# Expert blocks of 64 and of 128 rows in pairs, in the two-layer trunk's mixture of experts

## The chip, the cores and the metric

One Trainium2 chip, of which the kernel uses one core. The metric is the device time of one execution in microseconds (us), as the median of several; less is better. Its engines: TensorE (PE; PEld are its loads of stationary operands), VectorE (DVE), ScalarE (ACT), GpSimd (POOL) and SyncE (SP), which here only issues DMAs.

## The reference

Two layers over 1024 tokens of width 1024. In each, three mixers in parallel (a gated chunk mixer, a convolution, attention with latent keys) are normed and projected by W_o; then comes the mixture of experts, then a gated embedding per layer (gate W_g, projection e of p). All is float32. The change is in the mixture:

```python
t = m.reshape(-1, D)                       # 1024 tokens
g_idx = argmax(t @ wg + bg)                # 1 of 4 groups
topv, topi = top_k(softmax(elog of the group), 2)   # 2 of its 8 experts
flat_e = (g_idx[:, None] * 8 + topi).reshape(-1)    # 2048 choices, 32 experts
counts = bincount(flat_e, length=32)
padded = (counts + 127) // 128 * 128       # whole blocks of 128 rows
def expert_block(tok_b, w_b, e):           # for each block of 128 rows
    xb = t[tok_b]
    hb = silu(xb @ w_gate[e]) * (xb @ w_up[e])      # 1024 -> 256
    return (hb @ w_down[e]) * w_b[:, None]          # 256 -> 1024
```

On average an expert has 64 choices. The weights of one expert are three matrices of 1 MB. On the kernel's inputs the reference's routing gives, in layer 0, one expert with 134 choices, 16 with 65 to 117 and 15 with 25 to 62; in layer 1, 14 with 67 to 110 and 18 with 35 to 62.

## The kernel before

Every engine runs a program of its own, tied to the others by semaphores; the loop over the two layers is outside. A layer has the mixers, W_o with the norm and the router's logits, and then:

*Routing.* The end of W_o leaves the logits. VectorE computes the top two and the block lists in a chain of small instructions, each of which waits for the one before (`link`, L1417). TensorE counts choices per expert and ranks every choice by products with a triangle (L1915 to L1919), then turns the block counts into starts (`nb_col`, L1923). VectorE makes from them the block and the slot of each choice, 2 x 16 one-hot matrices (`hots`, L1487 to L1492), and TensorE multiplies these into the list of tokens of each block (L1932). The expert of each block is found on one partition by comparing the ends with a row of numbers, `le` and `owner` (L1499 to L1501). The cells of row 0 (`cells`) hold the owners, the number of blocks and running counts of the semaphores; the last is written at L1520. In the meantime TensorE works on e = p W_p in four calls of `project` (L1899); ScalarE copies e out and stores it in 16 DMAs over the two layers. SP, POOL, ACT, DVE and PE each wait for the cells and load five registers (`counters`, L455) before the blocks begin.

*Blocks.* All engines walk through the blocks with `block_loop` (L442), three to a lap, since weights and inputs have three slots. SP loads gate and up (L609, L610) into a slot as soon as gate_up of the block before the last but one is done and, after its down, the down weights (L614); the loads of the second block on also wait for the stores of e, whose buffer slot 1 takes. POOL gathers a block's rows of m by an indirect DMA (L783) into `x_blk` and scatters its output from `y_blk` into `choice_outputs` (L810); padding rows have an index out of bounds and are not moved. TensorE's order is written out by hand (L1982):

```python
guarded(pe, b < n, lambda: gate_up(m, *here))
guarded(pe, b + 1 < n, lambda: turn_x(m + 1, *nxt))
guarded(pe, b <= n, lambda: down(m - 1, *last))
guarded(pe, b < n, lambda: turn_h(m))
```

gate_up (L1957) is 8 products of 128 stationary columns (the block's rows) with 512 moving ones (gate and up), each of which the trace shows as two records; turn_x (L1948) is 8 transposes of the next block's rows; down (L1967) 4 products of 128 x 512 of the block before; turn_h (L1974) 2 transposes. ACT and DVE take the results out of PSUM: x in halves (L1048, L1527), silu and product (L1052, L1532, L1534), the hidden rows (L1056), y in halves (L1062, L1539). The evacuation of y waits until the store of the block before has landed, for there is one `y_blk`. After the blocks, SP waits for all stores, fetches each token's two rows, and the last part of the layer adds them to h.

## Time and profile before

| | |
|---|---|
| median of 3 runs | 2376.19 us (2371.58 to 2377.60) |
| profiled execution | 2380.11 us, span 2378.4 us |
| PE busy | 2184.1 us (92%), 8095 instructions |
| PEld / DVE / ACT / POOL busy | 1217.5 / 1100.9 / 594.8 / 369.1 us |
| mean granted clock of TensorE | 0.956 of full |
| DMA | 358.73 MB, mean 151 GB/s |
| experts' stages (first gate_up to last down) | 676 to 1056 us, and 1860 to 2229 us |

A matmul's record overlaps its neighbours, so busy time of a group is less than its count times the mean. A window of the trace gives each engine's busy time in it, the granted clock and the share of the 16 DMA engines' time, which can exceed 1 a little where packets overlap.

### The profile page before, as it was taken

What the parts mean: (1) busy time and instruction counts of PE and PEld (TensorE: products, weight loads), DVE (VectorE), ACT (ScalarE), POOL (GpSimd) and SP (SyncE); (2) the same over time, 40 slices, a digit from 0 to 9 for tenths busy, and PEclk for the clock granted to TensorE, in tenths of its full rate; (3) what the DMA queues carried; (4) which work ended last, traced back from release to release, by engine and by line L of the source; (5) the groups of instructions that cost most, each with busy time, mean ns of one, the idle gap of its engine ahead of it and who ended that gap; (6) DMA issues with size and microseconds to landing.
All of it is one profiled execution on the core that took longest, in us unless ns stands there. A gap on an engine that the chain in (4) does not pass through costs nothing.

```text
span 2378.4 us, 32689 instructions
## 1 busy us (share of the span) xinstructions
PE 2184.1 (92%) x8095; PEld 1217.5 (51%) x8095; DVE 1100.9 (46%) x2442; ACT 594.8 (25%) x1325; POOL 369.1 (16%) x545
## 2 busy tenths in 40 slices
PE   5999699999979999978979997999999799999698
PEld 2555477755534444434435554776555344444344
DVE  1488878754411121115425888787535121111253
ACT  2333233422211111111123332443213111111111
POOL 1222100011022222210013221000110222222100
PEclk9999799999889999998989997999998899999799
DMA  6011321001399999955300114210014999999422
GB/s 230 14 27 26 104 92 28 15 27 62 143 319 334 328 318 304 316 181 203 108 27 14 27 26 134 62 41 1 27 62 156 321 320 330 329 314 326 159 94 88
DMA packets 242022, 358.73 MB, mean 151 GB/s; under 512 B 22708, under 2 KB 190980, under 8 KB 241924
## 3 DMA queue, kind: packets, MB, share of 16 engines
q1 hardware_dynamic: 220900, 315.60, 39.7%
q0 software_dynamic: 18720, 33.60, 3.7%
q10 hardware_dynamic: 2304, 8.39, 0.9%
q8 instruction: 42, 0.69, 0.1%
q14 instruction: 56, 0.46, 0.1%
HBM read 324.48 MB, written 67.63 MB: 165 GB/s over the span
## 4 chain that ended last, share of the span: by engine, by line
PE 83%; DVE 6%; issue 5%; DMA 3%; ACT 1%; SPq 1%; DVEq 0%; POOL 0%; ACTq 0%; POOLq 0%
PE ps L1648 32%; PE ps L1957 19%; PE ps L1967 9%; PE ps L1805 4%; PE ps L1835 4%; PE ps L1617 2%; PE ps L1948 2%; PE ps L1819 2%; PE ps L1905 2%; PE ps L1737 2%; DMA h<-in_x_dram 1%; PE ps L1746 1%; DMA region_c<-in_moe_w_up_dram 1%; DVE neg_max L1355 1%; PE ps L1717 1%
## 5 line engine op out<-in xcount | busy, mean ns | idle before, releaser
L1648 PE MATMUL ps<-region_b,region_c 128*128 128x512 f32 x1024 | 453.3, 599 | 2.7 <-DVE region_c L1164 2.7
L1648 PE MATMUL ps<-region_a,region_c 128*128 128x512 f32 (+1 forms) x768 | 325.0, 578 | 14.9 <-ACT region_c L879 14.9
L1957 PE MATMUL ps<-region_c,region_a 128*128 128x512 f32 x704 | 314.4, 600 | 7.7 <-DMA region_c<-in_moe_w_up_dram 6.8
L1648 PEld LDWEIGHTS ps<-region_b,region_c 128*128 128x128 f32 x1024 | 194.1, 193 | 230.1 <-issue 229.6
L1532 DVE SCALAR_TENSOR_TENSOR region_a<-region_a,ps 128x256 f32<-128x256 f32 x65 | 27.4, 421 | 456.5 <-ACT region_a L1052 456.5
L1648 PEld LDWEIGHTS ps<-region_a,region_c 128*128 128x128 f32 x768 | 147.3, 195 | 175.8 <-issue 175.8
L1957 PEld LDWEIGHTS ps<-region_c,region_a 128*128 128x128 f32 x704 | 132.2, 193 | 159.0 <-issue 159.0
L1805 PE MATMUL ps<-region_c 96*128 96x512 f32 (+3 forms) x384 | 160.6, 530 | 0.0
L1967 PE MATMUL ps<-region_c,region_a 128*128 128x512 f32 x352 | 158.4, 593 | 0.7 <-DVE region_c L1539 0.7
L1957 PE MATMUL ps<-region_a 128*128 128x512 f32 x336 | 147.7, 592 | 0.0
L1835 PE MATMUL ps<-region_c,region_a 128*128 128x64 f32 x1152 | 146.8, 274 | 0.0
L1835 PEld LDWEIGHTS ps<-region_c,region_a 128*128 128x128 f32 x1152 | 143.1, 197 | 0.0
L1617 PE MATMUL ps<-ident,region_c 128*128 128x128 f32 x496 | 70.8, 292 | 76.0 <-DVE region_c L1148 60.0
L1052 ACT ACTIVATE region_a<-ps 128x256 f32<-128x256 f32 x65 | 25.0, 385 | 436.4 <-PE ps L1957 436.4
L991 ACT ACTIVATE region_a<-ps,neg_max 128x128 f32<-128x128 f32 (+7 forms) x128 | 94.9, 742 | 126.3 <-DVE neg_max L1355 124.8
L1539 DVE COPY region_c<-ps 128x512 f32<-128x512 f32 x65 | 44.9, 691 | 161.1 <-PE ps L1967 151.8
L1355 DVE TENSOR_REDUCE neg_max<-ps 128x1 f32<-128x128 f32 (+7 forms) x128 | 96.4, 754 | 45.9 <-PE ps L1808 45.1
L1617 PEld LDWEIGHTS ps<-ident,region_c 128*128 128x128 f32 x496 | 62.3, 150 | 101.4 <-DVE region_c L1148 73.5
L1819 PE MATMUL ps<-ident,region_a 128*128 128x128 f32 x576 | 89.1, 283 | 22.0 <-ACT region_a L991 22.0
L1957 PEld LDWEIGHTS ps<-region_a 128*128 128x128 f32 x336 | 62.2, 190 | 70.3 <-issue 70.3
L1967 PEld LDWEIGHTS ps<-region_c,region_a 128*128 128x128 f32 x352 | 63.6, 190 | 64.9 <-issue 64.9
L1819 PEld LDWEIGHTS ps<-ident,region_a 128*128 128x128 f32 x576 | 64.2, 145 | 52.4 <-ACT region_a L991 35.2
(292 smaller groups left out, 2810.3 us busy)
## 6 DMA issues: line engine op xcount, KB each, us to landing
region_c<-in_moe_w_gate_dram SPq DMA_DIRECT2D x44, 1024.0 KB, 9.1
region_c<-in_moe_w_up_dram SPq DMA_DIRECT2D x44, 1024.0 KB, 11.9
region_c<-in_moe_w_down_dram SPq DMA_DIRECT2D x44, 1024.0 KB, 5.7
region_a<-in_moe_w_gate_dram SPq DMA_DIRECT2D x21, 1024.0 KB, 9.7
region_a<-in_moe_w_up_dram SPq DMA_DIRECT2D x21, 1024.0 KB, 12.3
region_a<-in_moe_w_down_dram SPq DMA_DIRECT2D x21, 1024.0 KB, 5.6
region_c<-choice_outputs SPq DMA_DIRECT2D x32, 512.0 KB, 4.4
qk_heads<-gains SPq DMA_DIRECT2D x32, 384.0 KB, 4.2
```

Of the source, the lines that this page charges most:

```text
L991: nc.scalar.activation(prob[j % 2][:, 0:n], banks(2 * (j % 2))[:, 0:n], ACT.Exp, bias=neg_max[:, j % 2:j % 2 + 1], accum_out=denom[:, j:j ...
L1355: v.tensor_reduce(neg_max[:, j % 2:j % 2 + 1], banks(2 * (j % 2))[:, 0:(j + 1) * P], AX.X, ALU.max, negate=True).then_inc(*X_max.next(f"ma ...
L1617: ins = T(bank(b + k // 4, P * (k % 4), P * (k % 4) + P), src[:, P * k:P * k + P], ident[:, :])
L1648: ins = mm(dst, lhsT[:, k, :], w[:, k, a:b], start=(k == 0), stop=(k == KD - 1))
L1737: ins = mm(bank(half, 0, w), cnT[:, k, :], w_uq[:, k, w * half:w * half + w], start=(k == 0), stop=(k == 1))
L1805: mm(bank(b + c // 512, 0, w), q, k_ring[u][0:QK, c:c + w], start=True, stop=not last, skip_group_check=True)
L1819: ins = T(bank(4 + k // 4, P * (k % 4), P * (k % 4) + P), prob[j % 2][:, P * k:P * k + P], ident[:, :])
L1835: ins = mm(bank(6 + j % 2, 0, HEAD), prob_t[j % 2][:, k, :], vals[:, k, head, :], start=(k == 0), stop=(k == j))
L1905: ins = mm(bank(2 + 2 * u + half), pT[:, i, u, k, :], ple_p[:, k, 512 * half:512 * half + 512], start=(k == 0), stop=(k == 1))
L1948: ins = T(bank(k // 4, P * (k % 4), P * (k % 4) + P), x_blk[s][:, P * k:P * k + P], ident[:, :])
L1957: ins = mm(bank(2), xT[:, k, :], w_gu[s][:, k, :], start=(k == 0), stop=(k == KD - 1))
L1967: ins = mm(bank(4 + half), hid_t[:, k, :], w_dn[s][:, k, 512 * half:512 * half + 512], start=(k == 0), stop=(k == 1))
```

## The change

Each expert's choices are cut into full blocks (65 to 128 rows) and at most one small block (up to 64). Blocks are run in pairs, a small one first and then a full one; the number of pairs is half the number of blocks, rounded up, or the number of full ones if that is more. Small blocks beyond the number of pairs go into full places; places left over are void blocks with the weights of some expert and no rows to store that anyone reads. In a small block gate and up are computed with 64 stationary columns twice, `tile_position=(0, 0)` and `(0, 64)`: the two halves of the array's columns take 256 different moving columns each and write partitions 0 to 63 and 64 to 127. Down is split in the same way, the hidden rows need one transpose, and a small output is stored as 128 half rows from a buffer of its own, `y_half`; each of the two output buffers has its semaphore. The laps have six blocks. Owners come from three products on TensorE, placed between the halves of `project(1)`; SP starts the first loads after the owners, ahead of `counters`; slot 1 lies now where slot 2 was, so the third load waits for the stores of e. Block keys carry several fields that are cut out again with shifts and masks. The diff, cut to its core (ACT's and DVE's evacuations take `small` and half the width in the same way):

```diff
+            with eng.Fori(0, LAPS) as i:
+                def six():
+                    for u in range(6):
+                        b = 6 * i + (1 + u)
+                        step(b, ((1 + u) % 3, 2 * i + (1 + u) // 3), ((2 + u) % 3, 2 * i + (2 + u) // 3), (u % 3, 2 * i + u // 3),
+                             u % 2 == 0, 3 * i + u // 2)
+                guarded(eng, 6 * i < n, six)
...
-                prev, n, used = counters(sp, l, passed)
...
+                sp.wait_ge(*K_vec.after(l, "owner_i"))
+                settle(sp, passed)
                 for b in range(3):
-                    if b == 1:
+                    if b == 2:
                         for u in range(2):
                             sp.wait_ge(e_stored[u], 16 * PAIRS * l + 16 * PAIRS + 16)
                         settle(sp, passed)
                     load_dn(load_gu(b, b), b)
...
+                prev, n, half = counters(sp, l, passed, halves=True)
...
+                    rows = HALF if small else P
...
+                        out=x_blk[s][0:rows], out_offset=None, in_=m_dram,
+                        in_offset=bass.IndirectOffsetOnAxis(ap=idx_ring[0:rows, s:s + 1], axis=0),
...
+                gp.wait_ge(*K_vec.after(l, "rows_half"))
+                settle(gp, passed)
...
-                            in_=y_blk, in_offset=None, bounds_check=2 * SEQ - 1, oob_is_err=False).then_inc(y_stored, 16)
+                            out=y_halves if small else y_rows,
+                            out_offset=bass.IndirectOffsetOnAxis(ap=out_ring[:, k:k + 1], axis=0),
+                            in_=y_half if small else y_blk, in_offset=None, bounds_check=2 * VOID if small else VOID,
+                            oob_is_err=False).then_inc(y_stored[k], 16)
...
+                    act.wait_ge(y_stored[0 if small else 1], (half + i) * 16)
...
+                link(v.tensor_scalar(cnt[:, 1:2], cnt[:, 0:1], HALF - 1, None, ALU.add), "cnt_full")
+                link(v.tensor_scalar(cnt[:, 2:3], cnt[:, 0:1], P - 1, None, ALU.add), "cnt_all")
+                link(v.tensor_scalar(cnt[:, 3:5], cnt[:, 1:3], 7, None, ALU.logical_shift_right), "cnt_nb")
+                link(v.tensor_copy(nb_f[:, 0:2], cnt[:, 3:5]), "nb_f")
+                link(v.tensor_tensor(nb_f[:, 2:3], nb_f[:, 1:2], nb_f[:, 0:1], ALU.subtract), "n_half")
+                link(v.tensor_scalar(nb_cols[0:NE, 0], ones_b[0:NE, :], nb_f[:, 0:1], None, ALU.mult), "col_full")
+                link(v.tensor_scalar(nb_cols[0:NE, 1], ones_b[0:NE, :], nb_f[:, 2:3], None, ALU.mult), "col_half")
...
+                link(v.tensor_copy(ends, bank(6, 64, 64 + 4 * NE).rearrange("p (a e) -> p a e", a=4)), "start_f")
+                link(v.tensor_copy(cols[:, 0:2], ps[0:NE, 6, 192:194]), "cols_f")
+                link(v.tensor_tensor(both, n_full, n_half, ALU.add), "both")
+                link(v.tensor_scalar(quarter, both, 0.5, 0.25, ALU.mult, ALU.add), "quarter")
+                link(v.tensor_scalar(whole, quarter, ROUND, None, ALU.add), "whole")
+                link(v.tensor_scalar(n_pairs, whole, ROUND, n_full, ALU.subtract, ALU.max), "pairs")
...
+                link(v.tensor_scalar(cols[:, 2:3], cols[:, 1:2], n_pairs[0:NE], 0.0, ALU.subtract, ALU.max), "behind")
+                link(v.tensor_scalar(le[:, 0], nth_row, cols[:, 0:1], None, ALU.is_ge), "le_full")
+                link(v.tensor_scalar(le[:, 1], nth_row, cols[:, 2:3], n_full[0:NE], ALU.subtract, ALU.is_ge), "le_late")
+                link(v.tensor_scalar(le[:, 2], nth_row, cols[:, 1:2], None, ALU.is_ge), "le_half")
...
+                link(v.tensor_scalar(shift, n_full, n_pairs, -float(NE), ALU.subtract, ALU.subtract), "from_pairs")
+                link(v.tensor_scalar(keys[:, 0], start_half, n_pairs, shift, ALU.is_ge, ALU.mult), "moved")
+                link(v.scalar_tensor_tensor(keys[:, 1], end_full, 15.0, start_full, ALU.mult, ALU.add), "key_full")
+                link(v.tensor_tensor(keys[:, 2], start_half, keys[:, 0], ALU.add), "key_half")
+                link(v.scalar_tensor_tensor(keys[:, 3], keys[:, 2], 512.0, keys[:, 1], ALU.mult, ALU.add), "key")
...
+                link(v.tensor_scalar(dest, dest_f, float(SEQ), None, ALU.add), "dest_i")
...
+                for k, (name, right, mask) in enumerate((("slot", 0, P - 1), ("nth", 7, 7), ("is_half", 10, 1), ("end_full", 11, NE - 1),
+                                                         ("nr_half", 16, POS - 1))):
+                    link(v.tensor_scalar(fields_i[:, k], dest, right, mask, ALU.logical_shift_right, ALU.bitwise_and), name)
+                link(v.tensor_copy(fields, fields_i), "fields")
...
+                v.wait_ge(*K_pe.after(l, "owners"))
+                link(v.tensor_copy(owner, ps[0:1, 6, 256:256 + POS]), "owner_f")
+                link(v.tensor_scalar(cells[0:1, 0:POS].rearrange("p (r a) -> p a r", a=2), owner.rearrange("p (a r) -> p a r", a=2),
+                                     NE - 1, None, ALU.bitwise_and), "owner_i")
+                link(v.tensor_tensor(shared, fields[:, 3], fields[:, 1], ALU.add), "nr_full")
+                link(v.scalar_tensor_tensor(apart, fields[:, 4], -float(NE - 8), shared, ALU.add, ALU.subtract), "apart")
+                link(v.tensor_tensor(swap, apart, fields[:, 2], ALU.mult), "swap")
+                link(v.scalar_tensor_tensor(blk_f, swap, float(NE - 8), shared, ALU.add, ALU.add), "blk")
...
-                link(v.tensor_tensor(le, ends[0:1, 1].unsqueeze(1).to_broadcast([1, MAXB1, NE]),
-                                     iota[0:1, 0:MAXB1].unsqueeze(2).to_broadcast([1, MAXB1, NE]), ALU.is_le), "le")
-                link(v.tensor_reduce(owner, le, AX.X, ALU.add), "owner")
...
+                link(v.tensor_scalar(total, n_pairs[0:1], 2.0, None, ALU.mult), "n_blocks")
...
+                v.tensor_scalar(by_kind(idx), kinds, 3 * SEQ - 1, None, ALU.bitwise_and).then_inc(*K_vec.next("list_i"))
+                v.tensor_copy(cells[0:1, POS + 6:POS + 7], n_pairs[0:1]).then_inc(*K_vec.next("n_cell"))
+                v.tensor_copy(cells[0:1, POS + 4:POS + 5], total).then_inc(*K_vec.next("cells"))
+                v.tensor_copy(by_kind(out_idx)[:, 1], kinds[:, 1]).then_inc(*K_vec.next("rows_full"))
+                v.tensor_scalar(by_kind(out_idx)[:, 0], kinds[:, 0], 2.0, second[:, :], ALU.mult, ALU.add).then_inc(*K_vec.next("rows_half"))
...
-                pe.wait_ge(*K_vec.after(l, "nb_col"))
+                pe.wait_ge(*K_vec.after(l, "col_half"))
                 settle(pe, passed)
...
+                for k in range(2):
+                    a = 64 + 2 * NE * k
+                    mm(bank(6, a, a + NE), nb_cols[0:NE, k], tri_b[0:NE, 0:NE], start=True, stop=True)
+                    mm(bank(6, a + NE, a + 2 * NE), nb_cols[0:NE, k], tri_b[0:NE, 0:NE], start=True, stop=False)
+                    mm(bank(6, a + NE, a + 2 * NE), nb_cols[0:NE, k], ident_b[0:NE, 0:NE], start=False, stop=True)
+                mm(ps[0:NE, 6, 192:194], tri_b[0:NE, 0:NE], nb_cols[0:NE, :, 0], start=True, stop=False)
+                mm(ps[0:NE, 6, 192:194], ident_b[0:NE, 0:NE], nb_cols[0:NE, :, 0], start=False, stop=True).then_inc(*K_pe.next("starts"))
+                project(1, [0])
+                pe.wait_ge(*K_vec.after(l, "le_half"))
+                settle(pe, passed)
+                le = at(A, RS + 4608, 48).bitcast(BF16)[0:NE].rearrange("p (a r) -> p a r", a=3)
+                mm(ps[0:1, 6, 256:256 + NE], ones_b[0:NE, 0:1], le[:, 2], start=True, stop=True)
+                mm(ps[0:1, 6, 256 + NE:256 + POS], ones_b[0:NE, 0:1], le[:, 0], start=True, stop=False)
+                mm(ps[0:1, 6, 256 + NE:256 + POS], ones_b[0:NE, 0:1], le[:, 1], start=False, stop=True).then_inc(*K_pe.next("owners"))
+                project(1, [1])
                 project(2)
...
+                    mm(bank(6, 320 + NE, 320 + POS), hot_s[:, c, :], hot_b[:, c, NE:POS], start=(c == 0), stop=(c == 2 * TILES - 1))
+                for a in (0, HALF):
+                    for c in range(2 * TILES):
+                        ins = mm(ps[a:a + HALF, 6, 320:320 + NE], hot_s[:, c, 0:HALF], hot_b[:, c, 0:NE], start=(c == 0),
+                                 stop=(c == 2 * TILES - 1), tile_position=(0, a), skip_group_check=True)
                 ins.then_inc(*K_pe.next("lists"))
...
+                        ins = T(bank(k // 4, w * (k % 4), w * (k % 4) + w), x_blk[s][0:w, P * k:P * k + P], ident[0:w, 0:w])
...
+                        if small:
+                            pair = w_gu[s][:, k, :].rearrange("p (a f) -> p a f", a=2)
+                            for c in range(2):
+                                a = HALF * c
+                                ins = mm(ps[a:a + HALF, 2, 0:F].rearrange("p (a f) -> p a f", a=2), xT[:, k, 0:HALF],
+                                         pair[:, :, P * c:P * c + P], start=(k == 0), stop=(k == KD - 1),
+                                         tile_position=(0, a), skip_group_check=True)
+                        else:
+                            ins = mm(bank(2), xT[:, k, :], w_gu[s][:, k, :], start=(k == 0), stop=(k == KD - 1))
...
+                    if small:
+                        for j in range(2):
+                            for k in range(2):
+                                for c in range(2):
+                                    a, d = HALF * c, 512 * c + F * j
+                                    ins = mm(ps[a:a + HALF, 4 + j, 0:F], hid_t[:, 0, HALF * k:HALF * k + HALF], w_dn[s][:, k, d:d + F],
+                                             start=(k == 0), stop=(k == 1), tile_position=(0, a), skip_group_check=True)
+                            ins.then_inc(*M_dn.next(("lo", "hi")[j]))
+                        return
...
+                    for k in range(1 if small else 2):
...
+                    guarded(pe, b < n, lambda: gate_up(m, *here, not small))
+                    guarded(pe, b + 1 < n, lambda: turn_x(m + 1, *nxt, small))
+                    guarded(pe, b <= n, lambda: down(m - 1, *last, small))
+                    guarded(pe, b < n, lambda: turn_h(m, not small))
```

## Rows read from the trace of the kernel before

**Rows 1.** One block in the timeline of PE; then its turns of x, by form

```profile
722.27 7.03 PE L1957 MATMUL ps<-region_c,region_a 128*128 128x512 f32 x16
729.13 1.04 PE L1948 MATMUL ps<-ident,region_a 128*128 128x128 f32 x8
730.01 3.60 PE L1967 MATMUL ps<-region_c,region_a 128*128 128x512 f32 x8
733.44 0.38 PE L1974 MATMUL ps<-ident,region_a 128*128 128x128 f32 x2
733.66 6.60 PE L1957 MATMUL ps<-region_a 128*128 128x512 f32 x15
...
L1948 PE MATMUL ps<-ident,region_a 128*128 128x128 f32 x256 | 33.2, 273 | 0.0
```

**Rows 2.** Windows: the stage, both openings, the first 5 us of one

```profile
core 0: us, PE busy (x) PEld busy (x) DVE busy (x) ACT busy (x) POOL busy (x), PEclk, DMA share, GB/s
700.00:1020.00 320.00, 320.00 (x956) 156.05 (x955) 59.87 (x113) 53.99 (x113) 68.43 (x113) 1.00 0.94 321
666.00:700.00 34.00, 24.71 (x70) 12.55 (x71) 4.12 (x8) 3.81 (x8) 6.37 (x8) 0.80 1.05 373
1850.00:1884.00 34.00, 24.47 (x69) 12.46 (x70) 3.79 (x8) 3.48 (x7) 6.36 (x8) 0.80 1.05 363
671.00:676.00 5.00, 1.97 (x8) 1.56 (x8) 0.69 (x1) 0.59 (x1) 2.52 (x3) 0.50 1.05 390
```

**Rows 3.** Waits in the experts' stage of layer 0: total us, times, longest

```profile
ACT region_c L1062 <- DMA choice_outputs<-region_c,out_ring: 30.8, 13, 4.8
```

**Rows 4.** The page's DMA parts: a queue's packets, MB and share; issues with sizes

```profile
q0 software_dynamic: 18720, 33.60, 3.7%
...
region_c<-in_moe_w_up_dram SPq DMA_DIRECT2D x44, 1024.0 KB, 11.9
...
projected<-region_c ACTq DMA_DIRECT2D x16, 512.0 KB, 3.0
...
region_a<-moe_inputs,idx_ring POOLq DMA_INDIRECT x65, 7.4
```

**Rows 5.** SP's timeline: the first load of an expert in layer 0

```profile
660.71 0.38 SPq L609 DMA_DIRECT2D region_c<-in_moe_w_gate_dram  x1
```

**Rows 6.** Timeline of DVE, layer 0: counts, starts, owners, last cell

```profile
637.97 0.15 DVE L1464 CAST region_a<-ps 32x1 int32<-32x1 f32 x1 [3.11 <-PE ps L1919]
638.15 0.14 DVE L1465 TENSOR_SCALAR region_a<-region_a 32x1 int32<-32x1 int32 x1
639.33 0.23 DVE L1473 COPY region_a<-ps 128x64 f32<-128x64 f32 x1 [0.41 <-PE ps L1925]
...
649.07 0.30 DVE L1490 TENSOR_SCALAR region_a<-iota,region_a,token 128x48 f16<-128x48 f32 x1
651.06 1.74 DVE L1501 TENSOR_REDUCE region_a<-region_a 1x48 f32<-1x1536 f32 x1
...
656.17 0.13 DVE L1520 CAST cells<-region_a 1x1 int32<-1x1 f32 x1
```

**Rows 7.** Timeline of PE: the opening of the stage, and one piece of layer 1

```profile
639.22 15.70 PE L1905 MATMUL ps<-region_b,region_c 128*128 128x512 f32 x32
654.75 0.57 PE L1932 MATMUL ps<-region_a 128*128 128x48 f16 x16
...
671.00 1.97 PE L1948 MATMUL ps<-ident,region_a 128*128 128x128 f32 x8 [8.72 <-DMA region_a<-moe_inputs,idx_ring]
676.29 9.43 PE L1957 MATMUL ps<-region_c,region_a 128*128 128x512 f32 x16 [3.33 <-DMA region_c<-in_moe_w_up_dram]
...
1823.68 15.70 PE L1905 MATMUL ps<-region_b,region_c 128*128 128x512 f32 x32
```

**Rows 8.** Timeline of PE: the last down of each layer

```profile
1052.71 3.67 PE L1967 MATMUL ps<-region_a 128*128 128x512 f32 x8 [0.65 <-DVE region_c L1539]
...
2225.65 3.67 PE L1967 MATMUL ps<-region_c,region_a 128*128 128x512 f32 x8 [0.66 <-DVE region_c L1539]
```

272 lines of the change are left out of this document (142 added, 130 removed).

## The prediction

> **What bounds the kernel now.** I read the experts' stage, for only there does the change take work away. The timeline of TensorE comes first [rows 1]: one block of 128 rows is gate and up (6.87 us from its start to the next piece's), the next block's turn (0.87), down of the block before (3.43) and the turn of the hidden rows (0.22); the next block starts 11.40 us after this one, and no piece shows an idle time. The long window says the same of the whole stage: PE 320.00 us busy of 320.00 at a granted clock of 1.00, which is 2.4 GHz [rows 2]. So TensorE sets the pace, 11.40 us a block. The window's last columns are the second thing to see: the DMA engines are at 0.94 and move 321 GB/s. Right behind TensorE stands a resource that is nearly used up. How far it can go, the two openings show, where weights for several blocks are asked for at once: 373 and 363 GB/s at a share of 1.05 [rows 2]. Last, the evacuation of the output waited 13 times for the store of the block before, 4.8 us at most [rows 3]: one output buffer is near its limit too.
>
> **How many blocks.** The routing follows from the inputs. Worked out with the reference, layer 0 has 17 blocks that need 65 to 128 rows and 16 that need at most 64, layer 1 has 14 and 18. That is 33 + 32 = 65, as the 65 gathers say [rows 4]. In pairs they make 17 and 16 pairs: 33 small and 33 full, 66 blocks. One small block of layer 0 is void but still loads 3 MB of weights and runs. Two small blocks of layer 1 go through full places.
>
> **TensorE's term.** In a small block each product is split over two halves of the columns, 256 moving columns each. If the halves run side by side, gate and up cost 6.87 / 2 = 3.44 us and down 3.43 / 2 = 1.72. The turn of x still loads 8 x 2 sets of 128 columns; 8 records took 0.87 us, so nothing less is taken, and the hidden rows need one turn of two, 0.11. A small block is 3.44 + 0.87 + 1.72 + 0.11 = 6.14 us, a pair 11.40 + 6.14 = 17.5 us against 22.8. The trace has no matmul on half of the columns, so this is a bound: below stands full overlap (17.5), above none (11.28 for the small block, 22.7 a pair). Changing between whole and halved array about 7 times a pair costs from nothing to 7 x 0.17 us = 1.2 us (a turn's record lasts 273 ns [rows 1] where the next follows in 0.87 / 8 = 0.11 us; the difference is what is in flight). I take overlap, and 17.5 to 18.7 us a pair: the two halves read the same rows and write different partitions, and the weights' loads already run under matmuls (PEld 156.05 us busy in the 320.00 in which PE is always busy [rows 2]). The Trainium skill, TensorE: Matmul & The Clock Gate, "Measured speedup vs the span model", has three column tiles of 32 at 2.38 times one after another; no run here shows it, and by it I would trust the overlap rather more than less.
>
> **DMA's term.** The bytes don't shrink. A block's weights are 3 x 1.05 MB whatever its size, and the gathers and stores move only real rows already: 33.60 MB on their queue [rows 4], which is 2 x 2 x 2048 rows of 4 KB. A layer's weights are 34 x 3.146 = 107.0 MB (one void block more than before, +3.1) and 32 x 3.146 = 100.7 MB. A pair is 6.3 + 1.0 = 7.3 MB, so TensorE's 17.5 us would ask 417 GB/s, more than any long stretch reached. **So the bound moves from TensorE to the DMA engines.** For its rate: the steady mix, stores included, scaled to the full share, is 321 x 1.05 / 0.94 = 359 GB/s; the ends are 339 (the share doesn't rise) and 373 [rows 2]. The queue stays fed: when TensorE waits for a block's gate and up, its down, the next block whole and gate and up of the one after are already issued, 6 MB or 17 us.
>
> **When the DMA starts.** Before, the first weights were issued at 660.71 us [rows 5], 4.5 us after the last routing cell at 656.17 [rows 6], five register loads between. Now SP waits only for the owners, found by three products on TensorE. From the counts at 637.97 eight small steps instead of five, 0.18 us apart on 32 partitions [rows 6], bring the starts from 639.33 to 640.15; on 128 partitions I take 0.21 a step. Fifteen steps of that kind to the key (3.2 us), five over the 256 columns (0.46 each, 2.3), dest, five fields and their cast (1.5), two for the owners (0.4): owners at 647.5, first issue at 648.4, 12.3 us earlier. Data then flows from about 650.7. TensorE's three products stand inside project(1), between records of 0.43 us, at no cost; without that cover they would be 0.5 us. The chain to the cells grows: 26 steps more ahead of the one-hots (5.7 us), of which 5.4 were spare, since the lists waited for TensorE (one-hots done at 649.28, lists at 654.75 [rows 6, 7]); 48 small products instead of 16 (+1 us); the 1.74 + 1.74 us of the owners on one partition go, with two steps new. The cells come at about 657.9, +1.7. The gathers wait for them, behind POOL's registers, so the first turn moves from 671.00 to 672.7. Gate and up then start at about 675.6 instead of 676.29 [rows 7], where they waited for weights. POOL, ACT and DVE wait on the same cells, all before that turn. Moving the third load behind the stores of e only changes which buffer waits; they are next to be late, by 2 us at most, hidden under the first two blocks' loads. Evacuations of half the columns, the second output buffer and the memsets: nothing, beside 8 us or more of TensorE.
>
> **The sum.** From 650.7 to the landing of the last gate and up in layer 0, the engines carry 107.0 - 1.0 of weights, 15.8 of gathers and stores and 3.1 MB of six stores of e [rows 4] = 124.8 MB; at 359 GB/s 347.6 us, to 998.3. Behind that stand gate and up 6.9, the small down 1.7, a turn, two evacuations and the last down, 13.4 in all: 1011.7. Before it ended at 1052.71 + 3.67 = 1056.4 [rows 8]: -44.7 us. Layer 1 lies 1823.68 - 639.22 = 1184.5 us later [rows 7] and has 118.5 MB, 330.1 us: end 2178.6 against 2229.3, -50.7 us. Together -95 us. The profiled execution took 2380.1 us (span 2378.4), so 2284.7; from the median of the runs, 2376.2, which is 3.9 us lower, **2281 us**. At 373 GB/s it is -121 (2255), at 339 -55 (2321).
>
> **Rivals.** Where TensorE sets the pace, a layer ends at 675.6 + 3.9 + pairs x period; with 676.3 and 33 x 11.40 the same form gives the 1056.4 of before.
> (a) *TensorE stays the bound*, at a DMA rate above 390 GB/s. Periods of 17.5 and 18.7 us give -165 and -125; with the DMA at 385 GB/s -141. So about -130: 2246 us. For it: 5 us of the first opening moved 390 at a share of 1.05 [rows 2], nearly all of it weights. Against: neither stretch of 34 us did.
> (b) *The halves overlap in part*, or gathers come late. With half of the gain a small block is 8.7 us, a pair 21.1 with the changes of mode: -46, 2330 us. Gathers take 7.4 us to land [rows 4] and have about 10 in the shorter step; at over 10 this one holds too.
> (c) *The DMA engines give no more than now*, 321 GB/s, because 0.94 with stores is already full: 243.3 MB take 757.9 us, -15, 2361 us. The openings speak against it, but they had few stores.
> (d) *The halves do not run side by side* and it is slower. Then a small block is 11.28 us and the changes of mode are paid: 22.7 to 23.9 us a pair. Layer 0 ends 9 to 29 us later, layer 1 between 2 earlier and 17 later: +7 to +46, about 2403 us. It decides from a pair of 22.5 us on, that is, where less than 1.3 of the 10.3 us of products are hidden. The trace shows neither side, for nothing there runs on half of the columns. The skill has rules for it: TensorEngine Tiling, "Key Properties", lets a change of mode drain TensorE, and the TensorE page, "The mechanism", lets a load of weights run under a matmul only in another group of rows. Here both halves use all rows. On the whole array this trace disagrees with the second (156 us of loads under 320 of matmuls); what halves do, no run here shows.
>
> **How the numbers follow.** A measurement can tell 0.3%, 7 us, from no change. The forecast has 0.58, (a) 0.13, (b) 0.12, (c) 0.06, (d) 0.11. The first four are faster, less a little of (c); of (d) a small part is within 7 us: faster 0.87, same 0.03, slower 0.10. The range goes from 2240, which takes in most of (a), to 2345, beyond (b) and the 339 GB/s; (c), (d) and the best of (a) are left out.
>
> **What the profile after would show.** Right: gate and up of a small block in about 3.5 us with 32 records; TensorE idle ahead of gate and up, put down to the up weights' DMA, some 2 us a pair; a DMA share of 1.0 and about 360 GB/s through the stage; pairs 20 to 21 us apart; first weights near 648; clock still 1.00. Wrong: small products at 6.9 us (d), PE without idle time (a, b), or a rate that stays near 320 with TensorE waiting (c). A granted clock that falls to 0.50, 1.2 GHz, in the waits, as it had in the 5 us from 671 on, after 8.7 us without work [rows 2, 7], would double what follows and move this to (b) or worse.

## The result, and the profile after

The changed kernel takes **2307.64 us** (median of 4 runs, 2299.68 to 2308.32), against 2376.48 us for the kernel before beside it (4 runs, 2371.58 to 2377.60). The ratio is 0.9705, 95% interval 0.9686 to 0.9724: faster by 69 us, where 95 were forecast. The measured time lies inside the range. The profiled execution took 2307.06 us (span 2305.0), 73.0 less than the one before.

The page of the changed kernel, cut to its busy times, the GB/s of the 40 slices, two queues and the shares of the chain that ended last:

```profile
PE 2053.4 (89%) x8968; PEld 1180.5 (51%) x8968; DVE 1083.9 (47%) x2503; ACT 576.1 (25%) x1329; POOL 369.6 (16%) x550
...
GB/s 237 14 27 27 51 136 43 15 19 28 155 284 363 350 344 343 354 229 201 111 27 14 27 27 57 132 42 15 19 28 172 293 357 345 341 347 341 184 90 91
...
q1 hardware_dynamic: 223252, 318.74, 41.7%
q0 software_dynamic: 14784, 33.59, 4.1%
...
PE 64%; DMA 13%; DVE 8%; SPq 7%; issue 6%; ACT 1%; DVEq 0%; POOLq 0%; POOL 0%; ACTq 0%
PE ps L1735 33%; DMA region_c<-in_moe_w_up_dram 9%; PE ps L2071 5%; PE ps L1892 4%; PE ps L1922 4%; SPq L627 3%; PE ps L2067 3%; PE ps L1704 3%; PE ps L2092 2%; PE ps L1906 2%; SPq L623 2%; PE ps L1824 2%; DMA h<-in_x_dram 1%; PE ps L1833 1%; DVE neg_max L1389 1%
```

q0 moves as many bytes as before in fewer packets [rows 4], and q1 carries one void block more. What has grown is the second name of the chain's last line: 9% of the span are up weights on their way, against 1% before.

The timeline of PE for one pair that waits for nothing; it answers to [rows 1]:

```profile
679.75 7.11 PE L2071 MATMUL ps<-region_a 128*128 128x512 f32 x16 [0.67 <-DVE region_a L1609]
686.79 0.71 PE L2052 MATMUL ps<-ident,region_a 64*128 64x64 f32 x8
687.42 1.95 PE L2086 MATMUL ps<-region_c,region_a 128*64 128x256 f32 x16
689.30 0.44 PE L2099 MATMUL ps<-ident,region_a 128*128 128x128 f32 x2
689.67 3.67 PE L2067 MATMUL ps<-region_c,region_a 128*64 128x256 f32 x32
693.28 1.09 PE L2052 MATMUL ps<-ident,region_a 128*128 128x128 f32 x8
694.21 3.60 PE L2092 MATMUL ps<-region_a 128*128 128x512 f32 x8
697.64 0.27 PE L2099 MATMUL ps<-ident,region_a 128*128 128x128 f32 x1
697.75 2.74 PE L2071 MATMUL ps<-region_c,region_a 128*128 128x512 f32 x6
```

From 679.75 to 697.75 are 18.0 us. The small block's gate and up (L2067) go from 689.67 to the next piece at 693.28, 3.6 us with 32 records, and its down (L2086) takes 1.9, where the full ones take 7.0 and 3.4. The two halves run side by side.

The windows of layer 0's opening, of its stage up to the last gate and up, of a stretch of layer 1's opening, and of layer 1's stage; they answer to [rows 2]:

```profile
core 0: us, PE busy (x) PEld busy (x) DVE busy (x) ACT busy (x) POOL busy (x), PEclk, DMA share, GB/s
652.00:674.00 22.00, 13.47 (x86) 7.11 (x86) 5.28 (x29) 7.64 (x11) 8.74 (x13) 0.81 1.04 382
674.00:680.00 6.00, 5.33 (x36) 3.44 (x33) 1.26 (x3) 1.13 (x3) 1.00 (x1) 0.85 0.85 222
680.00:1007.74 327.74, 296.56 (x1456) 157.43 (x1456) 56.58 (x128) 51.35 (x128) 73.53 (x122) 0.98 1.04 351
...
1822.00:1828.00 6.00, 6.00 (x35) 3.79 (x31) 0.68 (x3) 0.82 (x2) 0.12 (x1) 0.65 0.66 206
1828.00:2142.91 314.91, 281.98 (x1366) 149.55 (x1366) 53.37 (x121) 48.23 (x121) 68.63 (x114) 0.97 1.05 347
```

And the waits of 700 to 1000 us for weights (total us, times, longest), here the two costliest rows:

```profile
PE ps L2071 <- DMA region_c<-in_moe_w_up_dram: 13.6, 7, 3.6
...
PE ps L2067 <- DMA region_c<-in_moe_w_up_dram: 11.6, 8, 2.5
```

TensorE, idle for none of 320 us before, is idle for 31 of 328, and nearly all of that is the wait for up weights. The DMA share has gone from 0.94 to 1.04 and 1.05. The bound has moved, as forecast. But the rate at that share is 351 and 347 GB/s in the two layers, not the 359 of the sum.

The ends and the opening, in the timelines of PE and SP, answer to [rows 5, 7, 8]. PE:

```profile
638.14 5.40 PE L1992 MATMUL ps<-region_b,region_c 128*128 128x512 f32 x8
643.47 0.17 PE L2021 MATMUL ps<-region_a,ones_b 32*1 32x32 bf16 x1
...
672.37 5.38 PE L2067 MATMUL ps<-region_c,region_a 128*64 128x256 f32 x32 [0.61 <-DVE region_a L1609]
...
1007.74 7.11 PE L2071 MATMUL ps<-region_c,region_a 128*128 128x512 f32 x16 [0.26 <-DMA region_c<-in_moe_w_up_dram]
...
1017.74 3.67 PE L2092 MATMUL ps<-region_c,region_a 128*128 128x512 f32 x8 [0.65 <-ACT region_a L1085]
...
1785.72 5.12 PE L1992 MATMUL ps<-region_b,region_c 128*128 128x512 f32 x8
...
2152.91 3.67 PE L2092 MATMUL ps<-region_a 128*128 128x512 f32 x8 [0.65 <-ACT region_a L1085]
```

SP, the first, second and third gate weights:

```profile
647.85 0.38 SPq L622 DMA_DIRECT2D region_c<-in_moe_w_gate_dram  x1
...
651.36 0.37 SPq L622 DMA_DIRECT2D region_a<-in_moe_w_gate_dram  x1
...
676.24 0.37 SPq L622 DMA_DIRECT2D region_c<-in_moe_w_gate_dram  x1
```

Layer 0's experts end at 1017.74 + 3.67 = 1021.4 us, 35.0 earlier than before. Layer 1's stage, measured from its own piece of `project` (1785.72; before 1823.68), ends after 370.9 us instead of 405.6: 34.7 less. Measured in the same way, layer 0's takes 383.3 us instead of 417.2, 33.9 less; the other 1.1 us passed ahead of it. The mixers between came out 3 us shorter, which no part of the change touches and which is chance: one group of their products (96x512, 192 records in layer 1) is busy for 77.5 us here and 80.3 before, and either value turns up in kernels with the same mixers (80.3 in e_moved and rows_of_2kb, 77.5 in long_rows). 35.0 + 34.7 + 3.0 is the 73 of the profiled executions.

### The profile page after: what moved, and what is told of

Same layout as the page of the kernel before. It is cut to its first block, busy times and chain, and to the rows that moved or that the text cites. A ratio compares the mean times of both kernels' runs of the same rounds, so it can differ in the third digit from the quotient of the medians.

```text
span 2305.0 us, 34453 instructions
## 1 busy us (share of the span) xinstructions
PE 2053.4 (89%) x8968; PEld 1180.5 (51%) x8968; DVE 1083.9 (47%) x2503; ACT 576.1 (25%) x1329; POOL 369.6 (16%) x550
## 4 chain that ended last, share of the span: by engine, by line
PE 64%; DMA 13%; DVE 8%; SPq 7%; issue 6%; ACT 1%; DVEq 0%; POOLq 0%; POOL 0%; ACTq 0%
PE ps L1735 33%; DMA region_c<-in_moe_w_up_dram 9%; PE ps L2071 5%; PE ps L1892 4%; PE ps L1922 4%; SPq L627 3%; PE ps L2067 3%; PE ps L1704 3%; PE ps L2092 2%; PE ps L1906 2%; SPq L623 2%; PE ps L1824 2%; DMA h<-in_x_dram 1%; PE ps L1833 1%; DVE neg_max L1389 1%
## 5 line engine op out<-in xcount | busy, mean ns | idle before, releaser
L1615 DVE SCALAR_TENSOR_TENSOR region_a<-region_a,ps 128x128 f32<-128x128 f32 x66 | 23.4, 354 | 442.0 <-ACT region_a L1080 424.3
L2071 PE MATMUL ps<-region_c,region_a 128*128 128x512 f32 x336 | 157.1, 623 | 28.3 <-DMA region_c<-in_moe_w_up_dram 28.3
L1892 PE MATMUL ps<-region_c 96*128 96x512 f32 (+3 forms) x384 | 155.2, 514 | 0.0
L1922 PEld LDWEIGHTS ps<-region_c,region_a 128*128 128x128 f32 x1152 | 142.0, 195 | 0.0
L1080 ACT ACTIVATE region_a<-ps 128x128 f32<-128x128 f32 x66 | 21.8, 330 | 419.6 <-PE ps L2071 270.8
L2071 PEld LDWEIGHTS ps<-region_c,region_a 128*128 128x128 f32 x336 | 65.1, 199 | 113.6 <-issue 113.6
L2067 PE MATMUL ps<-region_c,region_a 128*64 128x256 f32 x736 | 95.5, 418 | 22.2 <-DMA region_c<-in_moe_w_up_dram 21.0
L2071 PE MATMUL ps<-region_a 128*128 128x512 f32 x192 | 86.7, 605 | 9.0 <-DMA region_a<-in_moe_w_up_dram 7.7
L2067 PEld LDWEIGHTS ps<-region_c,region_a 128*64 128x64 f32 x736 | 63.0, 151 | 49.2 <-issue 30.7
L1892 PEld LDWEIGHTS ps<-region_c 96*128 96x128 f32 x384 | 65.6, 197 | 31.1 <-issue 30.6
L831 POOL COPY out_ring<-region_a 128x1 int32 x66 | 11.9, 180 | 421.3 <-DVE gains L1623 239.7
```

The lines of the kernel that those rows point to most:

```text
L1892: mm(bank(b + c // 512, 0, w), q, k_ring[u][0:QK, c:c + w], start=True, stop=not last, skip_group_check=True)
L1922: ins = mm(bank(6 + j % 2, 0, HEAD), prob_t[j % 2][:, k, :], vals[:, k, head, :], start=(k == 0), stop=(k == j))
L2067: ins = mm(ps[a:a + HALF, 2, 0:F].rearrange("p (a f) -> p a f", a=2), xT[:, k, 0:HALF], pair[:, :, P * c:P * c + P], start=(k == 0), stop= ...
L2071: ins = mm(bank(2), xT[:, k, :], w_gu[s][:, k, :], start=(k == 0), stop=(k == KD - 1))
```

## The experiments

My theory after the result: the halves overlap fully, TensorE has 2.5 us a pair to spare, and the DMA engines set the pace at about 350 GB/s, a pair in (1007.74 - 679.75) / 16 = 20.5 us. The rivals: the halves' gain comes from something else; gathers, stores or the buffer of e hold the weights up; the rate is a property of this mix of transfers and can be changed. All ratios are to the kernel before on the same chip, with 95% intervals; changes of code are against the changed kernel where nothing else is said. The experiments ran on several chips, on which the kernel before took 2372.2 to 2377.2 us, so a difference in us between the medians of two experiments is uncertain by some 4 us. Beside it I give what the two experts' stages together gained or lost in the traces, each measured from its own piece of `project` to the end of its last down (383.3 + 370.9 us in the changed kernel).

### Do the halves overlap, and what does it need?

**halves_in_turn** issues all products of one half before those of the other:

```diff
-for k in range(KD):
-    for c in range(2):
+for c in range(2):
+    for k in range(KD):
         ins = mm(ps[a:a + HALF, 2, 0:F]..., tile_position=(0, a))     # down likewise
```

> The changed kernel with one edit: in a small block all products of one half of the columns are issued, then all of the other, instead of alternating; the sums are the same. If the halves run side by side because neighbouring products lie on different halves, this takes the overlap away: gate and up of a small block go from 3.60 us to about 7.1, down from 1.88 to 3.6, a pair from 18.0 to about 23.3 us of TensorE's time, above what the DMA engines need; the experts' stages end about 54 and 48 us later, 2400 to 2412 us, slower than before the change. If the order doesn't matter (the halves overlap anyway, or the gain comes from elsewhere) it stays at 2307 us.

Measured 2314.96 us (2310.54 to 2319.39), 0.9748 (0.9730 to 0.9766). The expectation of a kernel slower than before was missed by far. The timeline of PE shows gate and up, and its neighbours:

```profile
715.10 6.31 PE L2065 MATMUL ps<-region_a 128*64 128x256 f32 x32
721.34 1.09 PE L2052 MATMUL ps<-ident,region_a 128*128 128x128 f32 x8
```

Gate and up take 6.24 us from start to start: two runs of 16 records overlap by little. Down, with runs of only 4 records a half, still takes 1.93 us, as in the alternating order. My reading is that a half's work starts past a few records of the other half that are still to run, and not past sixteen. A long run of full records takes 13.73 us for 32 in the changed kernel's trace, 0.43 each, so one of half the columns is 0.215, and 6.24 us are 29 of the 32; by that the reach is about 3 records. That number is worked out, not seen. With 20.63 us a pair TensorE is busy for all of the 260 us from 700 on and sets the pace itself, only just above the 20.5 us of the DMA engines, which is why the loss is only 7 us (the stages: 8.5).

**halves_apart** keeps that order and makes TensorE wait for the first half's last product before the second half's first:

```diff
+if c == 0:
+    ins.then_inc(*M_gh.next("g"))
+    pe.wait_ge(*M_gh.after(m))                 # down likewise, for each 512 columns
```

> The changed kernel with the two halves of the columns one after the other for certain: all products of one half, a wait for their end, then the other half, in gate and up as in down. If running side by side is what pays, the small block costs 3.5 us more in gate and up, 1.8 in down and some 0.6 for three waits: a pair 23.7 us instead of 17.93 of TensorE's time, layer 0 later by 61 us and layer 1 by 50, about 2418 us, and slower than before the change (2372 to 2376). If TensorE's time in small blocks doesn't matter beside the DMA, under 2330 us.

Measured 2391.60 us (2389.41 to 2392.75), 1.0067 (1.0046 to 1.0087): slower than before the change, by 0.7%. The timeline of PE has

```profile
712.64 3.41 PE L2090 MATMUL ps<-region_c,region_a 128*64 128x256 f32 x16
...
716.35 7.39 PE L2066 MATMUL ps<-region_a 128*64 128x256 f32 x32
723.67 1.09 PE L2053 MATMUL ps<-ident,region_a 128*128 128x128 f32 x8
```

7.32 and 3.34 us, and a pair takes 23.11 us (705.03 to 728.14), inside the 22.7 to 23.9 of rival (d), though 26 us short of my 2418. This is the rival's kernel, and it shows what the overlap is worth: 84 us (the stages: 85.2; the waits' own cost is in it), more than the whole gain.

### What holds TensorE up?

**up_eighth** loads only the first eighth of each up matrix, 1/8 MB instead of 1 MB; seven eighths of the up product use stale weights, and layer 1's routes differ.

```diff
-sp.dma_start(w_gu[s][:, :, F:2 * F], I["moe_w_up"][l, e].rearrange(...))
+sp.dma_start(w_gu[s][:, 0:1, F:2 * F], I["moe_w_up"][l, e][0:P].rearrange(...))
```

> The changed kernel loads only the first eighth of each up matrix (it computes with what is left in the buffer), 0.92 MB less a block. If the DMA engines bound the stage, TensorE's own pace appears: 18.0 us a pair, no idle time ahead of gate and up, the stage of layer 0 ends near 985 us instead of 1021. If something else held the pairs at about 20 us (gathers, stores, waits for evacuations) the stage still ends near 1021. The routing of layer 1 changes with the outputs, so only layer 0 is compared.

A single run, 2284.92 us. Layer 0 alone, whose routes are the same:

```profile
700.00:960.00 260.00, 260.00 (x1297) 135.75 (x1296) 50.93 (x114) 45.91 (x114) 70.20 (x116) 1.00 0.91 303
```

and its last down in the timeline of PE:

```profile
981.60 3.67 PE L2092 MATMUL ps<-region_c,region_a 128*128 128x512 f32 x8 [0.65 <-ACT region_a L1085]
```

It ends at 985.3, 36 us before the changed kernel, and a pair takes 17.93 us (702.78 to 720.71): TensorE's own pace, at the lower end of my 17.5 to 18.7. With fewer bytes nothing else stands in the way: not the gathers, the stores or the waits for evacuations.

**one_output** makes both kinds of block wait for the other's store as well, so that one buffer would do:

```diff
 act.wait_ge(y_stored[0 if small else 1], (half + i) * 16)
+act.wait_ge(y_stored[1 if small else 0], ...)                  # and on DVE
```

> The changed kernel in which each evacuation of y waits for the store of the block just before too, as with one output buffer. If the second buffer is needed at steps of 8 to 10 us (issue 2.2 us behind the evacuation and 7.5 or more to land), down waits and the time rises to 2315 to 2350 us. If the waits hide in the DMA-bound steps, it stays at 2302 to 2312 us.

2307.49 us (2302.00 to 2311.57), 0.9712 (0.9686 to 0.9738). The evacuations did wait for the other kind's store (ACT 16 times between 700 and 1000 us, 36.0 us in all), but TensorE did not wait for them: the second output buffer earns nothing at this pace.

**no_store_rows** stores two rows of the outputs and drops the others (filled once with other data at the start, since they are read later); layer 1's routes differ by that.

```diff
-bounds_check=2 * VOID if small else VOID,
+bounds_check=1,
```

> The changed kernel issues all stores of y, but nearly all rows are out of bounds and not moved (8.4 MB less a layer; the buffer in memory is filled once at the start instead). If a stored byte costs what a weight's byte does, at 350 GB/s, layer 0's stage ends 24 us earlier, near 997 us. If the scattered stores hold the engines for longer than their bytes, it ends at TensorE's pace, near 985 us. If the DMA engines don't bind, near 1021 us. Layer 1 is routed otherwise and not compared.

A single run, 2265.98 us. Layer 0's last down starts at 999.00 and ends at 1002.7, 18.7 us earlier (its stage is 18.0 us shorter), three quarters of the 24 us of the theory in which a stored byte costs what a weight's byte costs, and far from the 36 us of the one in which stores cost more. The window:

```profile
700.00:960.00 260.00, 241.94 (x1198) 127.37 (x1197) 46.22 (x104) 42.01 (x105) 64.06 (x107) 0.99 1.05 347
```

Without stores the rate is 347 GB/s at the same share of 1.05. So it isn't the stores that press the rate below 359.

### The opening

**cells_first** puts SP's loads behind its registers again, as before the change:

```diff
-sp.wait_ge(*K_vec.after(l, "owner_i"))
-settle(sp, passed)
+prev, n, half = counters(sp, l, passed, halves=True)
 for b in range(3):
```

> The changed kernel with SP waiting for the cells and their registers ahead of the first loads, as before the change. First load near 662.4 us instead of 647.9. If the stage is bound by the DMA engines from its first load on, each layer loses most of these 14.5 us, less the 4 to 5 us in which the engines now run dry after the second load: 8 to 12 us a layer, 2323 to 2331 us. If the opening is set by the gathers and TensorE, under 3 us a layer, at most 2313 us.

2320.92 us (2316.56 to 2322.03), 0.9773 (0.9757 to 0.9790). The first load is at 662.17 us and layer 0 ends 8.4 us later than with the change, 1.6 of which had passed before the stage; in all the early owners are worth 13 us (the stages: 6.8 + 6.7). It is less than two times the 14.3 us between the first loads, because the loads that start early run out of slots:

```profile
676.24 0.37 SPq L622 DMA_DIRECT2D region_c<-in_moe_w_gate_dram  x1
676.71 0.53 SPq L623 DMA_DIRECT2D region_c<-in_moe_w_up_dram  x1
```

(timeline of SP, the changed kernel: the third block's loads wait for the stores of e; the window from 674 to 680 above moved 222 GB/s, the 22 us before it 382.)

**e_moved** takes that wait away: e is copied out to other places, so the third load waits only for the last product of e.

```diff
-e_out = [at(C, 10240 + 1024 * u, D) for u in range(2)]
+e_out = [at(C, 12288, D), gains[:, FFN]]
...
-    for u in range(2):
-        sp.wait_ge(e_stored[u], ...)          # moved behind the third load, and to ACT's and DVE's first use
+    sp.wait_ge(*P_pe.before(TILES * l + TILES))
```

> The changed kernel with e's two output buffers in places that no slot of weights covers, so that SP's third load waits for TensorE's last product of e (662.6 us) and not for the stores of e (676.24). The engines ran dry then (158, 184 and 324 GB/s in three windows of 2 us). If the stage is bound by the DMA engines from the start, 2 to 5 us a layer: 2298 to 2304 us. If the dry stretch is refilled later, no change, 2305 to 2309 us.

2302.77 us (2302.09 to 2306.21), 0.9694 (0.9675 to 0.9713). The third load is issued at 664.52, the hole is half filled (290 GB/s from 674 to 680) and layer 0's last down starts 2.4 us earlier, at 1015.36 (0.6 of it passed before the stage). The two stages are 1.8 and 2.7 us shorter. Of the total, about 5 us lower, the interval overlaps that of the change: in the trace the gain is there, in the time it is not told apart.

### What sets the rate?

The gate and up matrices are fetched with rows `(k p) f`: every piece of a partition is one row of 256 floats, 1 KB. **long_rows** gives a partition eight neighbouring rows, one piece of 8 KB, and takes x's columns in the same order (stride 8) when it is turned, so that the sums are the same.

```diff
-w_gu = [s[:, 0:KD * 2 * F].rearrange("p (k f) -> p k f", k=KD) for s in slot]
+w_gu = [s[:, 0:KD * 2 * F].rearrange("p (a k f) -> p a k f", a=2, k=KD) for s in slot]
...
-sp.dma_start(w_gu[s][:, :, 0:F], I["moe_w_gate"][l, e].rearrange("(k p) f -> p k f", p=P))
+sp.dma_start(w_gu[s][:, 0], I["moe_w_gate"][l, e].rearrange("(p k) f -> p k f", k=KD))      # up likewise
...
-T(bank(...), x_blk[s][0:w, P * k:P * k + P], ident[0:w, 0:w])
+T(bank(...), x_blk[s][0:w].rearrange("r (p k) -> r k p", k=KD)[:, k], ident[0:w, 0:w])
```

> The changed kernel with gate and up loaded as 8 rows in a row for each partition (8 KB contiguous at both ends instead of 1 KB pieces); x is turned with a stride to match, the same bytes move. If 1 KB packets hold the rate at about 346 GB/s, the rate rises to 380 to 400 and the stages meet TensorE's pace of 18.0 us a pair: up to 35 us less a layer, 2240 to 2270 us. If the rate is a limit on bytes whatever the packets, it stays at 2302 to 2312 us.

**2261.54 us** (2258.65 to 2265.97), 0.9529 (0.9512 to 0.9547): 46 us below the change by the medians, 42 by the ratios and by the stages, some 60% as much again as the change itself brought. From its page and its windows:

```profile
q1 hardware_dynamic: 104980, 318.74, 38.7%
```

```profile
700.00:960.00 260.00, 249.12 (x1222) 133.05 (x1222) 48.12 (x108) 42.98 (x108) 65.36 (x108) 1.00 1.00 378
...
1890.00:2100.00 210.00, 202.07 (x999) 107.77 (x998) 38.56 (x88) 35.12 (x87) 51.79 (x85) 1.00 0.98 376
```

The same bytes in less than half the packets, and 378 GB/s at a share of 1.00. In layer 0 TensorE's waits for weights are gone (in layer 1 they are 6.0 us of the 210, against 23.5); what it waits for now is another thing. Its waits between 700 and 960, and one pair's two turns in its timeline:

```profile
PE ps L2052 <- DMA region_a<-moe_inputs,idx_ring: 10.9, 13, 1.2
```

```profile
707.43 1.09 PE L2052 MATMUL ps<-ident,region_a 64*128 64x64 f32 x8
...
714.94 1.13 PE L2052 MATMUL ps<-ident,region_a 128*128 128x128 f32 x8 [0.56 <-DMA region_a<-moe_inputs,idx_ring]
```

At this pace the gathers are late, as rival (b) had them, and the strided turn of a small block costs 1.03 us instead of 0.64. A pair takes 19.0 us, not the 18.0 that the expectation had as the end of the road.

**rows_of_2kb** is the same with pieces of 2 KB (`(q p k) f`, k = 2), to see whether the size of the piece is what counts and not the new layout.

> Between the changed kernel (1 KB pieces, 2307.6 us) and the one with 8 KB pieces (2261.5 us): gate and up in pieces of 2 KB, x turned with a stride of 2. If a piece has a fixed cost beside its bytes, 2 KB removes over half of it (pieces of a block 2048 -> 1024 for gate and up, against 256): the rate lies nearer to 378 than to 350 GB/s and the time at 2272 to 2288 us. If the gain comes only from long reads in memory (4 KB and more), it stays above 2295 us.

2273.76 us (2272.37 to 2278.86), 0.9566 (0.9550 to 0.9582), as expected between the two (the stages: 31.6 us shorter than with the change):

```profile
700.00:960.00 260.00, 249.63 (x1197) 135.09 (x1196) 46.66 (x105) 41.89 (x105) 65.36 (x108) 0.99 1.01 372
```

1 KB gives 350 GB/s in this window, 2 KB 372, 8 KB 378; TensorE is idle for 10.4 us of it with 2 KB, mostly for up weights, and for 10.9 with 8 KB, for gathers. From 2 to 8 KB only the size of the pieces changes, for 6 GB/s. The step from 1 to 2 KB also has the new layout in it (gate and up apart in the slot instead of side by side in each row), and no run has that layout with 1 KB pieces: that its 22 GB/s come from the size alone is argued, not shown. The Trainium skill, DMA: Bandwidth & Descriptors, "Why small descriptors are slow (HBM only)", has about 3 cycles of overhead per packet beside one for each 32 bytes; by that a 1 KB piece costs 35 cycles for 32, and I would estimate 4% for the whole mix at 8 KB, for gate and up are some 58% of the bytes. The trace agrees in direction and gives 8%.

**before_long_rows** makes the same edit in the kernel before, where TensorE is the bound.

> The kernel before the change, with gate and up loaded in 8 KB pieces as in the run with long rows. TensorE bounds it at 11.40 us a block and the DMA engines have room, so a better rate should bring nothing: 2365 to 2385 us (the strided turn may cost up to 0.4 us a block where the trace shows it, +5 to +25 us if it isn't free). If the DMA engines were already the bound before, it would gain as much as the changed kernel did, 46 us.

2377.29 us (2371.37 to 2378.39, 10 runs), 1.0001 (0.9988 to 1.0014), as expected. Its window:

```profile
700.00:960.00 260.00, 260.00 (x778) 128.08 (x777) 48.79 (x92) 42.09 (x91) 55.51 (x91) 1.00 0.87 321
```

The same 321 GB/s now cost a share of 0.87 instead of 0.94 [rows 2], and the time doesn't move. The longer pieces were worth nothing until the bound moved to the DMA engines.

**long_rows_ahead** gathers each block's rows one block earlier, ahead of a store on POOL's queue; **long_rows_ahead_e_moved** adds the moved buffers of e.

```diff
-gp.wait_ge(*M_xT.after(prev + b - 1))
-gather(b + 2, last[0], prev + b + 2, not small)
+gp.wait_ge(*M_xT.after(prev + b))
+gather(b + 3, here[0], prev + b + 3, small)          # and block 3 ahead of the loop
```

> The changed kernel with long rows, and POOL gathers the block three ahead in front of the store, one step earlier than before. With long rows TensorE waited 0.56 to 0.64 us for the gather once a pair. If that is the last bound, pairs go from 19.05 to about 18.4 us and the time from 2261.5 to 2240 to 2247 us. If the DMA engines bind again at about 380 GB/s (7.3 MB a pair: 19.2 us), the wait only moves to the weights: 2257 to 2265 us.

> The run before with e's output buffers moved as well. If TensorE sets the pace by now, filling the dry stretch brings at most 1 us a layer; if the DMA engines do, 2 to 5 us a layer.

2258.47 us (2255.79 to 2261.69), 0.9503 (0.9483 to 0.9523), and 2260.30 us (2257.08 to 2262.88), 0.9515 (0.9497 to 0.9532). The waits for gathers are gone and those for weights are back, fewer; the first of its two rows, and the window:

```profile
PE ps L2074 <- DMA region_c<-in_moe_w_up_dram: 4.2, 6, 1.1
```

```profile
700.00:960.00 260.00, 254.54 (x1256) 136.01 (x1256) 48.59 (x109) 43.59 (x109) 66.72 (x111) 1.00 1.00 383
```

A pair takes 18.37 us (700.63 to 719.00), which is TensorE's 17.93 with the strided turns, and TensorE is busy for 254.5 of the 260 us: it and the DMA engines are both near their limit. Layer 0's rate rises to 383 GB/s and its stage is 7.3 us shorter than in long_rows; layer 1's rate falls to 362 (at a share of 0.95), and its stage is 1.8 us longer, with TensorE's waits for up weights risen from 6.0 to 11.0 us of the 210. Why layer 1 goes the other way is not shown. With e's buffers moved the stages take the same time to 0.1 us, which is what was expected where TensorE sets the pace. In time neither kernel is told apart from long_rows. The three forms lie at 2258 to 2262 us, 42 to 49 us below the change and 111 to 119 below the kernel before on their own chips.

## Why the prediction was right in its mechanism and 27 us too low

**The bound moves from TensorE to the DMA engines: right.** Idle time of TensorE ahead of gate and up, put down to up weights, and a DMA share of 1.05 [windows above; before, rows 2]. up_eighth shows the counterpart: with fewer bytes the pace falls to 17.93 us at once.

**"I take overlap, and 17.5 to 18.7 us a pair": right.** 18.0 and 17.93 us. Gate and up came at 3.6 instead of 3.44, down at 1.88 instead of 1.72, and the small turn at 0.64 instead of the 0.87 I had refused to lower. Of the changes of mode, for which I had allowed up to 1.2 us, at most 0.6 can be there: 17.93 + 0.23 (what the small turn saved) - 17.54, all that the pieces of a pair take more than their terms. Two details under these terms were wrong: the timeline of a pair has five changes of the array's shape (from 128x128 to 64x128, 128x64, 128x128, 128x64 and back to 128x128), not seven, and the small turn loads 8 sets of 128 columns, not 8 x 2. Rival (d), slower, is refuted for this order; halves_apart shows that its price was right and its condition not met. The Trainium skill has two rules on which I built (d). TensorEngine Tiling, "Key Properties", lets a change of mode drain TensorE: the trace leaves at most those 0.6 us a pair to it. TensorE: Matmul & The Clock Gate, "The mechanism", lets a load run under a matmul only in another group of rows, though its first lines also speak of a background buffer for weights. Here both halves use all rows, and 32 records that would take 6.9 us one by one take 3.6, with their loads inside (from 855.00 to 858.60 us, one such piece, the matmuls are busy for 3.57 us and the loads for 2.64). So the measurement decides against the rule for halves of the columns.

**"At 359 GB/s 347.6 us, to 998.3": the step that failed.** The size of this term made 17.8 of the 25.7 us by which the two stages together came out longer than forecast. The sum scaled the steady rate of before by the shares, 321 x 1.05 / 0.94. The share did rise to 1.04 and 1.05, but with 351 and 347 GB/s. Layer 0 moved 327.74 us x 351 = 115.0 MB from 680 us to its last gate and up; at 359 that is 320.4 us, so 7.3 us were lost to the rate. In layer 1 it is 314.91 x 347 = 109.3 MB, 304.4 us at 359: 10.5 us. The 0.94 was not the room it looked. Both kernels load the weights in the same pieces, and yet at the full share a byte kept the engines busy for longer: 1.05 / 350 against 0.94 / 321, some 2.5% more, and 3.3% with layer 1's 347. That is this term's error. Why it does is not shown; it isn't the stores, for without them the rate was 347. That the share has no fixed price in GB/s is seen in before_long_rows too (0.94 against 0.87 for the same bytes). What a full share moves is told only by a stretch that has the same mix at the full share, and the openings of before, which had the share, were nearly without stores and short.

**"Owners at 647.5, first issue at 648.4": met, by luck.** The first load came at 647.85. But the counts, from which the chain of VectorE's steps starts, came 1.9 us earlier in this trace (L1499 at 636.03) than in that of before (637.97 [rows 6]), with nothing of the change ahead of them. From them to the first load it took 11.8 us instead of 648.4 - 637.97 = 10.4. (One sum in that chain was off as written: three more steps of 0.18 us are 0.54, where the starts were moved by 0.82; the trace has 0.86.) TensorE started gate and up at 672.37 instead of 675.6, which moves nothing where the DMA engines set the end.

**"They are next to be late, by 2 us at most, hidden under the first two blocks' loads": failed too.** The third load came only at 676.24, behind the stores of e, when the two first blocks had landed, and the DMA engines ran at 222 GB/s from 674 to 680: (359 - 222) x 6 / 359 = 2.3 us lost. Layer 1 has the same hole, with 206 GB/s from 1822 to 1828: 2.6 us. It was predicted to be late and called free, though in the new order nothing else was left to keep the queue busy. e_moved, which issues this load 12 us earlier, gets 1.8 and 2.7 us back.

**Layer by layer.** Layer 0 ended at 1021.4 where 1011.7 was forecast, 9.7 us later. 7.3 are the rate. Before 680 us it moved the other 124.8 - 115.0 = 9.8 MB in 680 - 650.7 = 29.3 us, where 359 GB/s asks 27.3: 2.0 us, about the hole. The tail behind the last gate and up's start took 13.7 instead of 13.4: 0.3. Layer 1 gained 34.7 instead of 50.7 us, 16.0 less: 10.5 are the rate, 0.3 the tail, and 5.1 the opening (its first data forecast 650.7 - 639.22 = 11.5 us behind the piece of `project`, so 1797.2; 30.8 us to 1828 for 118.5 - 109.3 = 9.2 MB, which ask 25.7). 2.6 of that are the hole. Of the other 2.5, 0.7 are a later first load, as SP's timeline has it:

```profile
1795.60 0.38 SPq L622 DMA_DIRECT2D region_c<-in_moe_w_gate_dram  x1
```

(by the forecast 648.4 - 639.22 = 9.2 us behind the piece of `project`, at 1794.9); 1.8 have no term. With the 3 us that the mixers came out shorter, this is the 22 us between the 95 forecast and the profiled executions' 73. The two medians lie 4 us closer to each other than the two profiled executions, which is the rest of the 27.

**The rivals.** (a), TensorE stays the bound, fell with its condition, a rate above 390 GB/s; none of the kernels held that over a stage. (b) fell for this kernel: no wait of TensorE for a gather stands in its two stages after the opening; its late gathers do appear in long_rows, where the pace is 19 us. (c), 321 GB/s, was half right in kind: the engines gave less than the openings promised, but 350. The clock did fall in the waits, as I had named at the end (PE's timeline):

```profile
759.80 8.80 PE L2071 MATMUL ps<-region_c,region_a 128*128 128x512 f32 x16 [2.25 <-DMA region_c<-in_moe_w_up_dram]
```

8.80 us instead of 7.0 for a full gate and up behind a wait of 2.25 us; the mean granted clock from 759.80 to 768.50 is 0.80, so it stood at 1.2 GHz for a part of it. Not every wait does this: behind 2.51 us the piece at 855.03 ran at 1.00. The mean granted clock of the stages is 0.97 to 0.98, where I had put 1.00, and in long_rows, which has only short waits, 1.00. Since TensorE has 2.5 us a pair to spare, I take it to cost next to nothing; no run measures it alone.

**The parts.** Undone one at a time: split columns are worth 84 us against the same pairs without overlap; early owners 13 us of the 69; the second output buffer nothing; slot 1's exchange with slot 2 was not tried alone.

**What stays open:** why a byte costs more at the full share than at 0.94; how much of the gain from longer pieces is the new layout; why layer 1's rate is a little lower in most kernels (347 against 351; the openings of before show it too [rows 2]); 1.8 us of its opening; whether a dropped gather would be paid like a dropped store, which was not run; and whether the reach of about 3 records is exact.

## What to carry to other kernels

When an engine at 100% is to be made faster, look at the share of the next resource: at 0.94 it allows little, and its last few per cent must be priced from a stretch with the same mix at the full share, not by scaling. After a bound has moved, take up again what was worth nothing before: the same edit of the weights' layout was worth 0 us on the old kernel and 42 to 46 on the new one. And a transfer that is "late but hidden" is free only while another one is there to fill the engines.

## What the runs showed of the hardware that was not expected

- Two column halves of TensorE with the same rows overlap nearly fully in float32 (32 records of 256 columns in 3.6 us; 7.32 with a wait between the halves), even without strict alternation where a half has 4 records in a row (1.93 us for 16), and almost not with 16 in a row (6.24 us).
- The DMA share is not a measure of GB/s: 321 GB/s stood at 0.94 with pieces of 1 KB and at 0.87 with 8 KB; at shares of 1.00 to 1.05 the engines moved 350 with 1 KB, 372 with 2 KB and 378 to 383 with 8 KB (the layout in the slot changed too between 1 and 2 KB).
- Turning x with a stride of 8 floats between columns costs 64 rows 1.03 us for 8 records instead of 0.64, and 128 rows next to nothing (0.97 from start to start, 0.93 without the stride). A stride of 2 costs both more: 1.10 and 1.06 us in rows_of_2kb.
